# A gated delta rule on 64 x 64 blocks: block matrices packed 64 wide in two partition halves, both directions alternating between halves of the matmul array

## The reference, cut to what matters

```
gc = cumsum(g);  decay = exp(where(lower, gc[..., :, None] - gc[..., None, :], -inf))
nil = where(strict, -einsum('nbhid,nbhjd->nbhij', kb, kc) * decay, 0)      # 64 x 64 per chunk and head
tinv = eye(64) + nil;  power = nil
for _ in range(5):
    power = power @ power
    tinv = tinv + tinv @ power
w_v = tinv @ (vc * beta);  k_cd = tinv @ (kb * exp(gc));  k_dec = kc * exp(g_last - gc)
# chunk after chunk:
v_new = w_v - k_cd @ state
out = qd @ state + (q k^T * decay) @ v_new
state = state * exp(g_last) + k_dec^T @ v_new
```

## Time and profile before

| | us |
|---|---|
| median of 3 runs | 3482.56 (3478.14 to 3482.67) |
| profiled execution | 3480.33 |
| its span in the trace | 3478.5 |
| mean granted TensorE clock | 0.969 of full |
| PE, weight loads, DVE, ACT, POOL busy | 3211.5, 2728.1, 1343.4, 1095.5, 1170.1 |

### The profile page before, as it was taken

The page is one execution under the profiler, slowest core; times in us unless marked ns, Lnnn a source line. Parts: engine busy times, 40 slices in busy tenths (PEclk is TensorE's granted clock), DMA queues, the critical chain, the costliest instruction groups (busy, mean ns, idle before and its releaser), DMA issues.

```text
span 3478.5 us, 49823 instructions
## 1 busy us (share of the span) xinstructions
PE 3211.5 (92%) x21019; PEld 2728.1 (78%) x21019; DVE 1343.4 (39%) x1765; ACT 1095.5 (31%) x1742; POOL 1170.1 (34%) x753
## 2 busy tenths in 40 slices
PE   5998999998889999799999989899999999989997
PEld 3887888876668888588888767789877778768885
DVE  4684434234561112422222368644424631232222
ACT  2442222223552212222222244432323542232222
POOL 4234333421203333323223232544531324444443
PEclk7999999999999999899999979999999999989999
DMA  5214433210002232122222121000111013423331
GB/s 196 67 33 155 158 111 104 67 53 20 9 6 64 64 100 67 34 65 61 67 61 61 55 73 43 25 1 1 49 55 31 10 51 99 136 62 97 97 93 59
DMA packets 303660, 231.41 MB, mean 67 GB/s; under 512 B 16784, under 2 KB 275280, under 8 KB 302544
## 3 DMA queue, kind: packets, MB, share of 16 engines
q1 hardware_dynamic: 297360, 204.55, 19.7%
q0 software_dynamic: 3776, 17.91, 1.4%
q10 hardware_dynamic: 2304, 5.77, 0.4%
HBM read 217.19 MB, written 11.98 MB: 66 GB/s over the span
## 4 chain that ended last, share of the span: by engine, by line
PE 82%; DVE 8%; issue 4%; ACT 3%; POOL 2%; DMA 0%; ACTq 0%; POOLq 0%; DVEq 0%
PE ps L409 19%; PE ps L410 19%; PE ps L411 19%; PE ps L653 3%; PE ps L668 3%; PE ps L494 2%; DVE stat L1188 2%; PE ps L515 1%; PE ps L713 1%; PE ps L700 1%; PE ps L532 1%; PE ps L421 1%; PE ps L717 1%; PE ps L701 1%; DVE R L1161 1%
## 5 line engine op out<-in xcount | busy, mean ns | idle before, releaser
L1536 POOL TENSOR_TENSOR wl<-wring,wh 128x1024 fp32r<-128x1024 f32 (+1 forms) x312 | 721.1, 2314 | 1368.2 <-ACT wh L922 1368.2
L409 PE MATMUL ps<-hh,wh 128*128 128x512 f32 (+1 forms) x2592 | 932.8, 360 | 90.1 <-DVE hl L1167 77.5
L410 PE MATMUL ps<-hl,wh 128*128 128x512 f32 (+1 forms) x2592 | 915.2, 353 | 0.0
L411 PE MATMUL ps<-hh,wl 128*128 128x512 f32 (+1 forms) x2592 | 914.4, 353 | 0.0
L409 PEld LDWEIGHTS ps<-hh,wh 128*128 128x128 f32 x2592 | 497.4, 192 | 179.1 <-issue 53.8
L410 PEld LDWEIGHTS ps<-hl,wh 128*128 128x128 f32 x2592 | 498.2, 192 | 67.8 <-issue 4.1
L411 PEld LDWEIGHTS ps<-hh,wl 128*128 128x128 f32 x2592 | 497.1, 192 | 66.3
L922 ACT ACTIVATE wh<-wring 128x1024 fp32r<-128x1024 f32 (+1 forms) x312 | 307.8, 988 | 523.6 <-PE ps L411 497.4
L1471 DVE SCALAR_TENSOR_TENSOR R<-ps,modcs,R 128x512 f32<-128x512 f32 x216 | 136.3, 659 | 387.7 <-PE ps L411 386.7
L410 PE MATMUL ps<-fl,wh 128*128 128x512 f32 (+1 forms) x768 | 274.8, 358 | 0.0
L411 PE MATMUL ps<-fh,wl 128*128 128x512 f32 (+1 forms) x768 | 274.5, 357 | 0.0
(11 more groups left out here) (232 smaller groups left out, 4791.2 us busy)
## 6 DMA issues: line engine op xcount, KB each, us to landing
wring<-in_w_ffn SPq DMA_DIRECT2D x128, 512.0 KB, 4.0
wring<-in_w_in SPq DMA_DIRECT2D x116, 512.0 KB, 3.8
wboth<-in_w_mod SPq DMA_DIRECT2D x80, 512.0 KB, 6.1
wring<-in_w_branch SPq DMA_DIRECT2D x48, 256.0 KB, 2.8
wring<-in_w_out SPq DMA_DIRECT2D x16, 512.0 KB, 3.8
x_store<-R POOLq DMA_DIRECT2D x2, 3072.0 KB, 9.6
R<-x_store POOLq DMA_DIRECT2D x2, 3072.0 KB, 11.6
R<-in_w_mod SPq DMA_DIRECT2D x7, 512.0 KB, 13.4
```

The lines of the kernel that those rows point to most:

```text
L409: mm(ps[:, t0:t1], ahk, rh[:, k, t0:t1], start=(k == 0), stop=False)
L410: mm(ps[:, t0:t1], ahk, rl[:, k, t0:t1], start=False, stop=False)
L411: last = mm(ps[:, t0:t1], alk, rh[:, k, t0:t1], start=False, stop=(k == kn - 1))
L1536: G.tensor_tensor(slot_view(wl, n % NSPL, l, name, i), w, slot_view(wh, n % NSPL, l, name, i).bitcast(F32), ALU.subtract)\
```

## The change

Each head's matrix is now kept as 64 columns instead of 128: rows 0 to 63 hold the block of the tile's first chunk, rows 64 to 127 that of the second. A product of such matrices is two products of 64 x 64, one with operands and result on partitions 0 to 63 and one on 64 to 127 (`halves`). Vector operations on these matrices go from 512 to 256 elements per partition. The transpose inside a power step is gone: the transposed power is computed as a second product (`halves(ps[:, 512:768], src, srcT)`), and both are copied before X. The recurrence works on the 64 rows of one chunk for each direction; in a step the two directions always stand in different halves, their products alternate, and the state is added before the output. POOL makes the masks ahead, and waits for less.

```diff
+            def halves(out, left, right):
+                for h in range(C_H):
+                    for lo in (0, HALF):
+                        last = mm(out[lo:lo + HALF, h * HALF:h * HALF + HALF], left[lo:lo + HALF, h, :],
+                                  right[lo:lo + HALF, h, :], start=True, stop=True)
+                return last
+            def delta_decays(l, s, d):
+                ...
+                for c, lo in enumerate((0, HALF)):
+                    mm(ps[:, 512 * c:512 * c + 256], ones[lo:lo + HALF, :], rows[c], start=True, stop=True)
+                for c, lo in enumerate((0, HALF)):
+                    last = mm(ps[lo:lo + HALF, 256:512], ones[lo:lo + HALF, 0:HALF], rows[c], start=True, stop=True)
...
                             ps = take(pe, "pw", l, s, d, i)
-                            for h in range(C_H):
-                                last = mm(ps[:, h * P:h * P + P], srcT[:, h, :], src[:, h, :], start=True, stop=True)
+                            last = halves(ps, srcT, src)
+                            if i < 4:
+                                last = halves(ps[:, 512:768], src, srcT)
                             last.then_inc(*filled("pw", l, s, d, i))
                         for d in range(2):
                             src, srcT, dst, dstT = power(d, i)
-                            if i < 4:
-                                pe.wait_ge(*read_first("pw", l, s, d, i))
-                                for h in range(C_H):
-                                    last = tr(pair("pw", l, s, d, i)[:, 512 + h * P:512 + h * P + P], dst[:, h, :], ident)
-                                last.then_inc(*pe_done.mark("pwT", l, s, d, i))
-                            else:
-                                pe.wait_ge(*read("pw", l, s, d, i))
+                            pe.wait_ge(*read("pw", l, s, d, i))
...
+                        new = [take(pe, "vn", l, n, d) for d in range(2)]
+                        for h in range(C_H):
+                            o = [new[d][at[d]:at[d] + HALF, h * P:h * P + P] for d in range(2)]
+                            for d in range(2):
+                                mm(o[d], cdbuf[d][:, chunk[d], h, :], S[:, 4 * d + h, :], start=True, stop=False)
+                            for d in range(2):
+                                ins = mm(o[d], xbuf[d][at[d]:at[d] + HALF, h, :], vbbuf[d][at[d]:at[d] + HALF, h, :],
+                                         start=False, stop=True)
...
                         for d in range(2):
                             pe.wait_ge(*read("vn", l, n, d))
                             pe.wait_ge(*pool_done.at("kd", l, s, d))
+                        so = [take(pe, "so", l, n, d) for d in range(2)]
+                        for h in range(C_H):
+                            for d in range(2):
+                                ins = mm(so[d][:, h * P:h * P + P], kbuf[d][at[d]:at[d] + HALF, h, :],
+                                         vnbuf[d][at[d]:at[d] + HALF, h, :], start=True, stop=True)
...
```

More of the change, by code:

```diff
@@ L695, in _ @@
                                 pe.wait_ge(*pool_done.at("vb", l, s, d))
[L696 to L701, removed]
@@ L1006, in _, with delta_decays @@
                 A(gex[:, :, 1, :], gtmp[:, :, :], ACT.Exp).then_inc(*act_done.mark("gex1", l))
+                def delta_decays(l, s, d):
+                    act.wait_ge(*read_first("bc", l, s, d))
+                    A(flat(wbuf[d]), flat(wbuf[d]), ACT.Abs).then_inc(*act_done.mark("abs", l, s, d))
+                    act.wait_ge(*act_done.at("abs", l, s, d))
+                    A(flat(wbuf[d]), flat(wbuf[d]), ACT.Exp, scale=-1.0).then_inc(*act_done.mark("W", l, s, d))
+                    A(qdbuf[s % 2][d].rearrange("p c h n -> p c (h n)"),
+                      pair("bc", l, s, d)[:, :].rearrange("p (c n) -> p c n", c=2)[:, :, 0:256], ACT.Exp)\
+                        .then_inc(*free("bc", l, s, d, by=1))
@@ L1007, in _ @@
                 for s in range(TT):
                     for d in range(2):
-                        act.wait_ge(*full("bc", l, s, d))
-                        if s:
-                            act.wait_ge(*full("vn", l, 2 * s - 1, d))
-                        A(flat(ebuf[d]), pair("bc", l, s, d)[:, 0:512], ACT.Exp).then_inc(*free("bc", l, s, d, by=1))
-                        act.wait_ge(*read("bc", l, s, d))
-                        A(flat(wbuf[d]), flat(wbuf[d]), ACT.Abs).then_inc(*act_done.mark("abs", l, s, d))
@@ L1016, in _ @@
[L1016 to L1017 removed]
+                        delta_decays(l, s, d)
                     for d in range(2):
[L1019 to L1020 removed]
+                        delta_queries(l, s, d)
                     for d in range(2):
[L1022 removed]
@@ L1023, in _ @@
-                        A(flat(tbuf[d]), pair("AT", l, s, d)[:, 0:512], ACT.Copy).then_inc(*free("AT", l, s, d))
+                        delta_turned(l, s, d)
                     for i in range(5):
@@ L1615, in _ @@
-                        pool.wait_ge(*read("G", l, s, d))
-                        pool.wait_ge(*dve_done.at("gb", l))
-                        G.tensor_tensor(wbuf[d], ktok[:, t, :].rearrange("p (h n) -> p h n", h=C_H),
-                                        along(gex[:, t, 0, 4 * d:4 * d + 4]), ALU.mult)\
-                            .then_inc(*pool_done.mark("kbe", l, s, d))
-                    for d in range(2):
-                        t = tiles[d][s]
-                        pool.wait_ge(*full("pw", l, s, d, 4))
+                        pool.wait_ge(*full("kcd", l, s, d))
```

293 lines of the change are left out of this document (169 added, 124 removed).

## The result

| | before | after |
|---|---|---|
| median of the runs, us | 3480.92 (20 runs) | 3496.2 (20 runs) |
| ratio, 95% interval | | 1.0039 (1.0025 to 1.0053) |
| profiled execution, its span, us | 3480.33, 3478.5 | 3494.09, 3492.2 |
| mean granted clock | 0.969 | 0.937 |

The account below looks back on a forecast made before the run. PE's matmuls were taken to bound the kernel; period gains 6 x 5.1 + 4 x 5.8 + 2 x 2.7 = 59, say 60 us, took 3480.3 to 3420, a median of 3422 us, 1.7% faster. Range 3348 to 3500.

Parts of the forecast that it names:

- a term that stood among the rivals with a chance of 0.05: Granted clock at half for a fifth of the stages, 7.4 us a period lost, 3511 us; chance 0.05.
- Halves overlap, 0.027 from start to start: In `halves` products on PE, small records start every 0.027 us, a group of 16 costing 0.43.
- The rival's 0.055: `halves` products take turns in one PSUM bank, 0.88 us a group, 156 us more, 3578 us; chance 0.18.
- the case in between (0.030 to 0.037): Small records start every 0.030 to 0.037 us, giving 3440 to 3482 us; chance 0.07.
- A power step of 3.8 us with 1.1 idle that DVE's copy ends: Steps i = 0..3 take 3.8 us instead of 4.46, PE idling 1.1 in each; gain 2.6 a period.
- A change of shape, 0.2 us: Changing PE's tile shape, as every four records in `vn`, costs 0.2 us from last start to next.
- The rival that it costs nothing: Shape changes in `vn` and output are free, 1.76 us each instead of 3.3, 66 less, 3356 us; chance 0.15.
- The new wait before the state products, 1.4: In the recurrence PE idles 1.4 us, since ACT's two copies of 0.59 follow both directions' `vn`.
- The transition, 7.7: From first decay product to first power, 7.7 us instead of 9.27 in a layer 1 period; gain 1.6.
- A period of 46.6 us in layer 1, 56.8 in layer 0: Whole delta-stage periods with outputs: layer 1 gains 5.8 us from 52.36, layer 0 gains 5.1 from 61.85.
- A clock of 1.00: The granted clock was to stay at 1.00, the longest idle time foreseen being 1.7 us.
- the two signs by which I would have called the forecast wrong: Forecast wrong if a power step is longer than 4.46 us, or a `vn` pair takes 1.8.

Follow-up runs that it names:

- e6_copies_first: e1_grouped with DVE copying both transposed powers out before it adds either X in a power step; 3356.02 us.
- e1_grouped: The changed kernel with the products of `vn` and output in two groups per chunk, 128-row ones first, then 64-row ones, instead of in turns; 3386.91 us.
- e5_before_changes: The kernel before, with each head's second product in `vn` and output cut to the chunk's 64 rows, so the shape alternates every two records; 3592.56 us.
- e7_both_shorter: e6_copies_first with DVE copying `vn` of direction 1 while ACT copies that of direction 0; 3342.39 us.
- e2_filler: The changed kernel with three extra 128 x 256 products, whose results are overwritten, issued before PE waits for the two `vn` copies; 3427.40 us.
- e8_before_waits: The kernel before, with the state products of each direction waiting for the `vn` copies of both; 3500.70 us.
- e9_before_both: The kernel before with the edits of both e5_before_changes and e8_before_waits; 3816.90 us.

## Why the prediction was wrong

The forecast was 60 us faster; the kernel came out 15 us slower. The sum was right to some 10 us, by an estimate from the price of the clock (3411 to 3427 beside 3420); the sign was lost to a term that stood among the rivals with a chance of 0.05. Step by step:

- **Halves overlap, 0.027 from start to start: near.** (3.02 - 0.22)/95 = 0.0295. The rival's 0.055 falls, and with it the worry about one PSUM bank. The Trainium skill's TensorEngine Tiling (Array Packing), Gotcha 1: PSUM Pressure, has different row tiles unable to access one bank simultaneously; for halves that differ in columns too, no such limit is seen here: their records, 0.22 us long, start 0.0295 apart in one bank. 0.0295 lies next to the lower edge of the case in between (0.030 to 0.037): 0.0025 more for each of 16 records is 0.04 us a group, some 14 us over 30 groups in 12 periods.
- **A power step of 3.8 us with 1.1 idle that DVE's copy ends: right.** It is 3.95 (2469.31 to 2473.26) with 0.93 idle, and e6_copies_first took that idle time out.
- **A change of shape, 0.2 us: right.** A group of four in `vn` is 0.37 instead of 0.41 at full clock, a pair 2.94 instead of 3.3. The rival that it costs nothing falls: e1_grouped removed 0.89 of each pair. In the old kernel e5_before_changes paid 113 us for 704 changes, 0.16 each.
- **The new wait before the state products, 1.4: right**, 1.50, ended by ACT's two copies. From `kcd` to `vn` I had 2.9; it is 3.02 (375.74 to 378.76), but POOL ends it, not the copies that I named. In the last recurrence of a layer ACT's weight tile makes the wait 2.45 and 2.58 (2492.62, 2503.75), 1.0 and 1.1 more; 1.05 was forecast.
- **The transition, 7.7: mis-sized.** From `bc` at 2459.51 to the first power at 2465.83 it is 6.3. I took 0.055 for the records of `G` and `Q`; a run of 48 of them at full clock takes 1.63 us in e7_both_shorter, (1.63 - 0.22)/47 = 0.030.
- **A period of 46.6 us in layer 1, 56.8 in layer 0: near, at full clock only.** The three stretches at full clock add up to 44.7 us for a layer 1 period with outputs, 1.9 less than forecast, by the transition and by `kcd` and the recurrence (20.1 instead of 21.3). With 0.3 us taken off for each us at half clock, 47.89 becomes 46.2 by estimate, the one without output 44.42 becomes 41.2 (42.9 forecast), and 60.19 in layer 0 becomes 58.8. Gains by these estimates: 6 x 3.1 + 4 x 6.2 + 2 x 4.4 = 52, where 59 was the sum. Layer 0 falls short by 2 us a period. In the period of 60.19 PE had 2.5 us of idle time that nothing in the profile explains, before a modulation and in a power step; what it is stays open.
- **A clock of 1.00: wrong, and this is the step that failed.** From the earlier trace rows I had taken that a long idle time lowers the clock; it is even longer there than the 3.6 us that I read, since it runs on into the next stretch: the timeline has 5.04 before the record at 941.40. Against the rival stood only that the longest idle time would be 1.7. That was no argument: in the old recurrences no such wait stands beside the changes of shape, and where the attention stage has both, 4 to 28 records stand between two changes, so the old trace did not show what a change every four records does with waits. Neither of the two signs by which I would have called the forecast wrong, a step over 4.46 and a `vn` pair of 1.8, came up; both speak of PE's records, not of the clock. Its half clock for a fifth of the stages became a third (241 of some 670 us), and its 7.4 us a period became 6.0. The forecast's two own terms, 0.2 for each change of shape and 1.4 for the new wait, were each paid as priced and then again by the clock: 67 us by the lower price (83 by the higher), which took the gain of 52 (69) and some 15 more.

That both together lower the clock is shown by e1_grouped, e2_filler, e5, e8 and e9. What the chip measures to decide it is not: no run separates the time for which the array drains from the idle time as one quantity, and the same recurrence kept its clock at one place (2439.42 to 2459.51) and lost it at another. The Trainium skill's TensorE: Matmul & The Clock Gate, A second HAM failure mode: psum-queue depth-cycling, tells of a clock that swings between its levels when the engine pauses briefly and often between groups of matmuls; the 1.01 before the fall at 380 us agrees, and e8_before_waits adds that 24 pauses of 0.79 us did nothing where the array's shape mostly stayed.

## What to carry to other kernels

Price a change on TensorE at both clock levels: where it adds changes of the array's shape and waits of about 1 us or more in one place, read the granted clock by stretch before trusting the sum, and take one of the two away (group products of one shape, split an eviction over two engines, or fill the wait). Small block products in different row and column halves pay if the halves alternate record by record. Where all engines are less busy and the span is longer, look at the clock first: two periods with the same record counts and different lengths show it at once.

## What the runs showed of the hardware that was not expected

- The clock fell to 0.50 after idle times of 1.01 (changed kernel) and 0.79 us (e9_before_both), each next to changes of shape every 2 to 4 records; in the old kernel the changes alone, or waits of 0.79 alone, left it at 0.99 to 1.00 from 276 to 600 us. With 8 to 28 records between two changes even waits of 1.50 and 2.96 left it at 1.00 (827 to 849 us, kernel before).
- At half clock a group of four records with its change of shape takes 0.62 instead of 0.37, and a us at half clock cost the kernel 0.3 to 0.4 us by the periods and the 19 executions of the changed kernel, and 0.44 in e9_before_both (203 us for 464 more at half than in e5); the waits for other engines stay as long (0.93, 1.50).
- 64 x 64 products that alternate between halves in one PSUM bank start every 0.0295 us; half after half 0.038, not the 0.055 of the earlier trace rows.
- Products with 128 rows, 64 array columns and 64 moving columns start every 0.030 us, those with 128 moving columns every (1.09 - 0.27)/15 = 0.055.
